# Split activations for TensorE: from high and low parts side by side to one block of low parts and one block of high parts

## The chip, the cores and the metric

The kernel runs on one core of a Trainium2 chip. The metric is the device time of one execution in microseconds. Before the change the median of three runs is 1348.29 us (1348.04 to 1348.34). A profiled execution took 1349.55 us, and the rows below are of that one.

## The reference

A sequence of 256 tokens with 1024 features goes through one layer of a first network and two layers of a second one, all in float32, batch 1. Cut to the parts that hold the large products:

```python
# first network, one layer
h = rmsnorm(x, g_mix);  z = h @ w_in            # 1024 -> 3232, split into latents, q, k, v, gates
ya, yb = two attentions over z ...              # projected by w_oa, w_ob
x = x + (sigmoid(gate_a) * ya + sigmoid(gate_b) * yb) @ w_o
u = relu(rmsnorm(x, g_mlp) @ w_up);  x = x + (u * u) @ w_down        # 1024 -> 4096 -> 1024
x = x + sigmoid(rmsnorm(x, g_ple) @ w_ple_gate) * (p @ w_ple)
x = rmsnorm(x, g_final)
# second network, two layers; the feed-forward runs before and after each mixer
def swiglu(h, w_in, w_out):
    a, b = split(h @ w_in, 2);  return (silu(a) * b) @ w_out         # 1024 -> 2 x 2816 -> 1024
for layer in range(2):
    x = x + 0.5 * swiglu(rmsnorm_2(x), ...)
    x = x + (even_mixer or odd_mixer)(rmsnorm_2(x), ...)
    x = x + 0.5 * swiglu(rmsnorm_2(x), ...)
out = rmsnorm_2(x, final_norm_g)
```

## The kernel before, in words

Products keep float32 accuracy with TensorE's fp32r type in three passes. Every weight block is loaded in float32 into `raw` by the SP queue, rounded by ScalarE into a high part `whi` (line 1278) and the rest is written by VectorE as a low part `wlo` (line 1734). Four slots of 2048 columns of each are held. Activations are split alike, into high parts (`hh`) and low parts (`hl`), and a product is the sum of high times high, high times low and low times high; low times low is left out.

The activations that enter the wide layers are held transposed, in the tile `hx`: eight blocks k of 128 features, 256 tokens each. Before the change the high part of block k is followed at once by its low part, so that both are one run of 512 columns: `hx` is `[128, 8, 2, 256]`. ScalarE writes the high parts (lines 1304, 1464 and 1540), VectorE the low ones (lines 1764, 1998 and 2126). The tiles are placed one after the other in each partition: `whi` and `wlo` begin at a multiple of 512 B, `hx` 64 B behind one (the tile `pad_hx` of 16 floats, line 204), and `ra`, which holds other activations, at a multiple of 512 B again (`pad_ra`).

TensorE's program is written out by hand, in one order, with waits on semaphores; each matmul is issued by `mm` (line 466), the transposes by `tp` (line 475). A matmul has a stationary operand (128 by 128, loaded by an LDWEIGHTS of its own) and a moving operand (128 rows by 128 to 512 columns). `hx` is read in three ways:

- `up_part` (lines 502 to 520), for the layers 1024 to 4096 and 1024 to 2 x 2816. For each of two groups f of 128 outputs and eight blocks k, a **wide pass** keeps a block of `whi` stationary and moves high and low parts of block k together, 512 columns, into the PSUM bank of f. Then, for the same f and k, a **correction pass** keeps the block of `wlo` stationary and moves the high part alone, 256 columns, onto the columns of the bank that hold the high products. VectorE adds the bank's two halves of 256 columns with a reduction (`hi_and_lo`, line 1834). A call of all eight blocks has 16 wide and 16 correction passes. With `behind=1` (the second of two calls in a feed-forward step) the last wide pass stands behind the correction passes.
- `gemm_b`, `b_part`, `by_steps` and two short loops: a **triple** of passes with weights stationary, moving 256 columns each: `whi` with `hh`, `whi` with `hl`, `wlo` with `hh`.
- `gemm_a` and its like: `hx` is stationary, in a triple `hh`, `hh`, `hl`, and weights move, mostly 512 columns.

A step of a feed-forward layer is one or two calls of `up_part`, then `down`: 24 passes with a piece of `ra` stationary and 512 columns of weights moving. In these layers wide passes, correction passes and `down` follow each other all the time. The split of later weights, the reductions and the activation functions run on the other engines beside them.

Of the kernel before, what the change touches and what calls it, by code (L numbers as in the profile page):

```python
# [7 lines left out]
R = mybir.dt.float32r  # L8
# [4 lines left out]
S = 256  # L13
# [150 lines left out]
def program(nc, W, XIN, XT, PT_IN, CST, GNS, GQK, GFIN, GFIN2, GLAG, FOXB, T5, OUT):  # L164
# [22 lines left out]
    with ExitStack() as ctx:  # L187
        def sb(name, shape, dt=F):
            return ctx.enter_context(nc.sbuf_tensor(name, shape, dt))
# [5 lines left out]
        ps = [pp[:, i, :] for i in range(8)]  # L195
# [5 lines left out]
        sb("pad", [128, 120])  # L201
        whi = sb("whi", [128, NHL, CW], R)
        wlo = sb("wlo", [128, NHL, CW], R)
        sb("pad_hx", [128, 16])
        hx = sb("hx", [128, 8, 2, S], R)
        sb("pad_ra", [128, 112])
        ra = sb("ra", [128, 4096], R)
        raw = sb("raw", [128, NRAW, HW])
        X = sb("X", [128, 2, D])
# [66 lines left out]
        def two(a):  # L276
            return a.rearrange("p (h c) -> p h c", h=2)

        def flat(a):
            return a.rearrange("p r c -> p (r c)")  # L280
# [20 lines left out]
            i, c, n = halves[j]  # L301
            return wlo[:, i % NHL, c:c + n]

        hh, hl = hx[:, :, 0, :], hx[:, :, 1, :]
        xT = fx[:, :].rearrange("p (k c) -> p k c", k=8)
        ACC = [[0, 1], [2, 3]]
        accs = [[ps[b][:, :] for b in r] for r in ACC]
# [156 lines left out]
        def tensor_program(pe):  # L464
            def mm(o, lhs, rhs, first, last):
                return pe.matmul(o, lhs, rhs, start=first, stop=last, skip_group_check=True)  # L466
# [35 lines left out]
            def up_part(tag, b, ks, norm=None, behind=0):  # L502
                i = IDX[tag]
                s = i % NHL
                wide = [(f, k) for f in range(2) for k in ks]

                def both(f, k, last):
                    c = k * 256 + f * 128
                    return mm(ps[b + f][:, :], whi[:, s, c:c + 128], flat(hx[:, k, :, :]), k == 0, last)

                for f, k in wide[:len(wide) - behind]:
                    if f == 0 and norm is not None:
                        pe.wait_ge(s_hl, 8 * norm + k + 1)
                    both(f, k, False)
                for f, k in wide:
                    c = k * 256 + f * 128
                    y = mm(ps[b + f][:, 0:256], wlo[:, s, c:c + 128], hh[:, k, :], False, k == 7 and not (behind and f))
                for f, k in wide[len(wide) - behind:]:
                    y = both(f, k, k == 7)
                return y  # L520
# [58 lines left out]
            def opening(k, tags):  # L579
                ta, tb = tags  # L580
                pe.wait_ge(s_hl, 8 * k + 4)
                weights_ready(IDX[ta])
                if k == 3:
                    pe.wait_ge(s_pgt, 2)
                up_part(ta, 4, range(4))
                if k == 3:
                    weights_ready(IDX[tb])
                    pe.wait_ge(s_pgt, 4)
                    up_part(tb, 6, range(2))
                    join_turn(k, 1)  # L590
                    up_part(tb, 6, range(2, 4))
                else:
                    weights_ready(IDX[tb])
                    up_part(tb, 6, range(1))
                    join_turn(k, 1)
                    up_part(tb, 6, range(1, 4))
                up_part(ta, 4, range(4, 8), k).then_inc(s_done)
                if k not in (1, 3):
                    spread(k, 0)
                up_part(tb, 6, range(4, 8)).then_inc(s_done)  # L600
                if k == 3:
                    spread(k, 0)
# [2015 lines left out]
```

## Time and profile before

| | before |
|---|---|
| median of 3 runs | 1348.29 us |
| the profiled execution, its own time | 1349.55 us |
| its span from first to last instruction | 1347.5 us |
| granted TensorE clock, mean over the span | 0.997 |
| TensorE (PE) busy | 1331.7 us, 99% |
| weight loads (PEld) busy | 1143.9 us, 85% |
| VectorE (DVE) busy | 968.7 us, 72% |
| ScalarE (ACT) busy | 678.6 us, 50% |
| GpSimd (POOL) busy | 68.6 us, 5% |
| mean DMA rate | 179 GB/s |

How to read it: a matmul's start is recorded and its end is modelled, and matmuls overlap, so the mean duration of one (some 390 ns for 512 columns) is not what a pass costs. What it costs is the distance from its start to the start of the next. The timeline gives that: it merges equal neighbours, so a row with `x16`, and the start of the row behind it, give the time of 16 passes.

### The profile page before, as it was taken

The page shows a single profiled execution, that of the slowest core. Times are in us where ns is not written, and L with a number is a line of the kernel's source. Part 1 is how long each engine was busy: PE and PEld are TensorE (multiplying, and loading weights), DVE is VectorE, ACT ScalarE, POOL GpSimd, SP SyncE. Part 2 cuts the span into 40 slices and gives each one's busy share as a digit, 9 for nine tenths or more (in the row PEclk, how much of TensorE's full clock was granted, in tenths as well). Part 3 has the DMA queues.
Part 4 walks back from the last instruction along what each step waited for, and adds up shares of the span by engine and source line. Part 5 has one row for each costly group of instructions (what it writes and reads, how often), then busy time and mean ns, then how long its engine had stood idle before and what let it go on. Part 6 is the DMA issues. An engine that isn't in the chain of part 4 may idle for free.

```text
span 1347.5 us, 19411 instructions
## 1 busy us (share of the span) xinstructions
PE 1331.7 (99%) x7680; PEld 1143.9 (85%) x7680; DVE 968.7 (72%) x1325; ACT 678.6 (50%) x1058; POOL 68.6 (5%) x108
## 2 busy tenths in 40 slices
PE   8999999999999999999999999999999999999998
PEld 6988888888888888898888888888888887888886
DVE  6786777666687776657767777777676798676775
ACT  6587354444564444556654444544443667544442
POOL 0300010000000000004000000000000043000000
PEclk9999999999999999999999999999999999999999
DMA  9353546555536656564346555556555555566551
GB/s 336 113 167 116 184 163 232 196 193 190 187 121 217 198 194 195 160 203 120 133 156 218 189 195 193 173 191 200 194 196 167 176 146 147 173 204 204 188 188 47
DMA packets 67562, 241.24 MB, mean 179 GB/s; under 512 B 7983, under 2 KB 8376, under 8 KB 67472
## 3 DMA queue, kind: packets, MB, share of 16 engines
q1 hardware_dynamic: 65200, 234.19, 52.8%
q0 software_dynamic: 1984, 5.70, 1.8%
q8 instruction: 61, 1.00, 0.3%
q14 instruction: 29, 0.24, 0.1%
q10 hardware_dynamic: 288, 0.11, 0.0%
HBM read 238.88 MB, written 1.09 MB: 178 GB/s over the span
## 4 chain that ended last, share of the span: by engine, by line
PE 90%; DVE 6%; issue 1%; ACT 1%; DMA 1%; POOL 0%; DVEq 0%; POOLq 0%; SPq 0%; ACTq 0%
PE pp L466 87%; DVE wlo L1734 2%; PE pp L475 2%; DVE fa L1734 1%; DVE hx L1742 0%; DMA raw<-w_chunks 0%; DVE pbuf L1738 0%; ACT whi L1278 0%; DVE fa L1834 0%; DVE xn L1734 0%; ACT hx L1279 0%; DVE xn L1943 0%; DMA fa<-f_rows 0%; DVE fa L1742 0%; DMA f_rows<-fa 0%
## 5 line engine op out<-in xcount | busy, mean ns | idle before, releaser
L1734 DVE TENSOR_TENSOR wlo<-raw,whi 128x1024 fp32r<-128x1024 f32 (+1 forms) x444 | 523.1, 1220 | 139.0 <-ACT whi L1278 138.7
L466 PE MATMUL pp<-hx,whi 128*128 128x512 f32 (+1 forms) x2400 | 546.8, 360 | 2.1 <-DVE fa L1834 1.1
L1278 ACT ACTIVATE whi<-raw 128x1024 fp32r<-128x1024 f32 (+1 forms) x444 | 442.0, 1043 | 80.3 <-PE pp L466 72.9
L466 PEld LDWEIGHTS pp<-hx,whi 128*128 128x128 f32 x2400 | 419.5, 188 | 72.2 <-issue 7.9
L466 PE MATMUL pp<-whi,ra 128*128 128x512 f32 x1144 | 365.9, 391 | 0.5 <-issue 0.5
L466 PE MATMUL pp<-hx,wlo 128*128 128x256 f32 x2032 | 311.8, 277 | 0.0
L466 PEld LDWEIGHTS pp<-hx,wlo 128*128 128x128 f32 x2032 | 276.3, 188 | 10.1
L466 PEld LDWEIGHTS pp<-whi,ra 128*128 128x128 f32 x1144 | 214.6, 188 | 44.1 <-issue 1.6
L466 PE MATMUL pp<-wlo,ra 128*128 128x512 f32 x572 | 222.6, 389 | 0.0
L1834 DVE TENSOR_REDUCE fa<-pp 128x512 f32<-128x1024 f32 x104 | 127.0, 1221 | 72.6 <-PE pp L466 72.4
L1278 ACT ACTIVATE ra<-fa 128x512 fp32r<-128x512 f32 x63 | 39.8, 632 | 227.6 <-DVE fa L1742 227.6
L1374 ACT ACTIVATE fa<-fa 128x512 f32<-128x512 f32 x44 | 27.8, 632 | 194.6 <-DVE fa L1734 194.6
L466 PEld LDWEIGHTS pp<-wlo,ra 128*128 128x128 f32 x572 | 107.5, 188 | 21.3 <-issue 0.2
L466 PE MATMUL pp<-whi,hx 128*128 128x512 f32 (+2 forms) x320 | 95.6, 378 | 2.0 <-DVE wlo L1734 2.0
L1734 DVE TENSOR_TENSOR ra<-fa,ra 128x512 fp32r<-128x512 f32 x63 | 43.6, 693 | 43.3 <-ACT ra L1278 43.3
L2405 POOL TENSOR_TENSOR st<-st,cst 128x2 f32<-128x2 f32 (+3 forms) x15 | 13.4, 894 | 1180.7 <-DVE st L1739 1159.4
L466 PEld LDWEIGHTS pp<-whi,hx 128*128 128x128 f32 x320 | 58.8, 190 | 15.8 <-issue 4.1
L466 PE MATMUL pp<-wlo,hx 128*128 128x512 f32 (+2 forms) x160 | 60.1, 375 | 0.0
L1742 DVE SCALAR_TENSOR_TENSOR fa<-fa 128x512 f32<-128x512 f32 x65 | 44.5, 684 | 2.8 <-ACT fa L1625 0.7
L1742 DVE SCALAR_TENSOR_TENSOR hx<-pp,gns,hx 128x256 fp32r<-128x256 f32 x64 | 26.5, 477 | 23.1 <-ACT hx L1279 23.1
L1317 ACT ACTIVATE xn<-X 128x512 f32<-128x512 f32 x36 | 22.4, 627 | 28.4 <-DVE X L1742 28.1
L466 PEld LDWEIGHTS pp<-wlo,hx 128*128 128x128 f32 x160 | 30.5, 191 | 5.6
(176 smaller groups left out, 767.3 us busy)
## 6 DMA issues: line engine op xcount, KB each, us to landing
raw<-w_chunks SPq DMA_DIRECT2D x438, 512.0 KB, 5.2
fa<-t_rows POOLq DMA_DIRECT2D x16, 128.0 KB, 3.5
fx<-x_t SPq DMA_DIRECT2D x2, 512.0 KB, 6.5
X<-x_in SPq DMA_DIRECT2D x2, 512.0 KB, 7.4
fa<-g_fin POOLq DMA_DIRECT2D x2, 512.0 KB, 4.3
fa<-f_rows POOLq DMA_DIRECT2D x8, 128.0 KB, 3.2
raw<-w_chunks SPq DMA_DIRECT2D x3, 256.0 KB, 5.8
cst<-consts POOLq DMA_DIRECT2D x1, 576.0 KB, 7.4
```

The costliest lines, as they stand in the source:

```text
L466: return pe.matmul(o, lhs, rhs, start=first, stop=last, skip_group_check=True)
L475: return pe.transpose(o, src, ident[0:n, 0:n])
L1278: return act.activation(o, i, ACT.Copy, scale=1.0)
L1317: act.activation(xn[:, t, sl], X[:, t, sl], ACT.Square, scale=1.0, accum_out=st[:, q + 2 * c + t:q + 2 * c + t + 1]).then_inc(s_sq)
L1374: act.activation(fr[:, g % 2, :], fr[:, g % 2, :], ACT.Silu, scale=1.0).then_inc(s_silu)
L1734: return dve.tensor_tensor(o, a, b, op)
L1742: return dve.scalar_tensor_tensor(out=o, in0=a, scalar=s, in1=b, op0=op0, op1=op1)
L1834: return dve.tensor_reduce(two(o), pp[:, b:b + 2, :].rearrange("p f (s c) -> p f c s", s=2), AX.X, ALU.add)
L2405: return pool.tensor_tensor(o, a, C("mhalf")[:, 0:1].to_broadcast([128, n]), ALU.pow)
```

## The change

`hx` becomes `[128, 2, 2064]`: a block of all eight low parts (2048 floats), 16 floats of padding, then a block of all eight high parts. `pad_hx` goes and `pad_ra` shrinks by 16 floats, so that the block of low parts begins at a multiple of 512 B, the block of high parts 64 B behind one, and `ra` and all tiles behind it stay where they were. `hl` and `hh` become views of the two blocks. A wide pass now moves two runs of 256 columns, low part first, 8256 B apart, where it moved one run of 512. So the high products land in columns 256 to 511 of a bank, and the correction passes add onto these; the reduction adds the halves as before. No instruction is added, removed or moved on any engine. Where ScalarE and VectorE write two neighbouring blocks in one instruction (lines 1540 and 2126), two runs of 256 become one of 512.

```diff
--- before.py
+++ after.py
@@ -201,9 +201,8 @@
         sb("pad", [128, 120])
         whi = sb("whi", [128, NHL, CW], R)
         wlo = sb("wlo", [128, NHL, CW], R)
-        sb("pad_hx", [128, 16])
-        hx = sb("hx", [128, 8, 2, S], R)
-        sb("pad_ra", [128, 112])
+        hx = sb("hx", [128, 2, 8 * S + 16], R)
+        sb("pad_ra", [128, 96])
         ra = sb("ra", [128, 4096], R)
@@ -301,7 +300,7 @@
-        hh, hl = hx[:, :, 0, :], hx[:, :, 1, :]
+        hl, hh = [hx[:, i, 0:8 * S].rearrange("p (k c) -> p k c", k=8) for i in range(2)]
@@ -506,7 +505,7 @@
                 def both(f, k, last):
                     c = k * 256 + f * 128
-                    return mm(ps[b + f][:, :], whi[:, s, c:c + 128], flat(hx[:, k, :, :]), k == 0, last)
+                    return mm(two(ps[b + f][:, :]), whi[:, s, c:c + 128], hx[:, :, S * k:S * k + S], k == 0, last)
@@ -514,7 +513,7 @@
                 for f, k in wide:
                     c = k * 256 + f * 128
-                    y = mm(ps[b + f][:, 0:256], wlo[:, s, c:c + 128], hh[:, k, :], False, k == 7 and not (behind and f))
+                    y = mm(ps[b + f][:, 256:512], wlo[:, s, c:c + 128], hh[:, k, :], False, k == 7 and not (behind and f))
```

## Rows read from the trace of the kernel before

**Rows 1.** The page: busy time by engine, and the chain that ended last.

```profile
PE 1331.7 (99%) x7680; PEld 1143.9 (85%) x7680; DVE 968.7 (72%) x1325; ACT 678.6 (50%) x1058; POOL 68.6 (5%) x108
...
PE 90%; DVE 6%; issue 1%; ACT 1%; DMA 1%; POOL 0%; DVEq 0%; POOLq 0%; SPq 0%; ACTq 0%
```

**Rows 2.** Groups by form on PE: passes with `hx` (count; mean, idle before).

```profile
L466 PE MATMUL pp<-hx,whi 128*128 128x512 f32 x1664 | 408.8, 393 | 1.4 <-DVE fa L1834 1.1
...
L466 PE MATMUL pp<-hx,wlo 128*128 128x256 f32 x2032 | 311.8, 277 | 0.0
L466 PE MATMUL pp<-hx,whi 128*128 128x256 f32 x736 | 138.0, 287 | 0.7 <-DVE fx L1734 0.7
L466 PE MATMUL pp<-whi,hx 128*128 128x512 f32 x256 | 83.6, 401 | 2.0 <-DVE wlo L1734 2.0
```

**Rows 3.** Timeline of PE, a feed-forward step (start us, modelled us, what).

```profile
399.21 3.60 PE L466 MATMUL pp<-hx,whi 128*128 128x512 f32 x15
402.65 1.98 PE L466 MATMUL pp<-hx,wlo 128*128 128x256 f32 x16
404.46 0.39 PE L466 MATMUL pp<-hx,whi 128*128 128x512 f32 x1
404.69 0.39 PE L466 MATMUL pp<-whi,ra 128*128 128x512 f32 x1
...
405.60 0.39 PE L466 MATMUL pp<-wlo,ra 128*128 128x512 f32 x1
...
409.68 0.39 PE L466 MATMUL pp<-wlo,ra 128*128 128x512 f32 x1
...
410.14 3.84 PE L466 MATMUL pp<-hx,whi 128*128 128x512 f32 x16
413.82 1.98 PE L466 MATMUL pp<-hx,wlo 128*128 128x256 f32 x16
```

**Rows 4.** Timeline of PE: 16 correction passes at another price, and the next 16.

```profile
539.71 2.05 PE L466 MATMUL pp<-hx,wlo 128*128 128x256 f32 x16
541.59 3.61 PE L466 MATMUL pp<-hx,whi 128*128 128x512 f32 x15
545.04 1.98 PE L466 MATMUL pp<-hx,wlo 128*128 128x256 f32 x16
546.85 0.39 PE L466 MATMUL pp<-hx,whi 128*128 128x512 f32 x1
```

**Rows 5.** Timeline of PE: the last full series of 16 correction passes in the program.

```profile
1322.53 1.98 PE L466 MATMUL pp<-hx,wlo 128*128 128x256 f32 x16
1324.34 0.39 PE L466 MATMUL pp<-hx,whi 128*128 128x512 f32 x1
```

**Rows 6.** Timeline of PE: `ra` stationary, then triples that move `hx`.

```profile
60.07 0.39 PE L466 MATMUL pp<-whi,ra 128*128 128x512 f32 x1
60.30 0.40 PE L466 MATMUL pp<-hx,whi 128*128 128x256 f32 x2
...
61.01 0.40 PE L466 MATMUL pp<-hx,whi 128*128 128x256 f32 x2
...
62.07 0.40 PE L466 MATMUL pp<-hx,whi 128*128 128x256 f32 x2
```

**Rows 7.** Timeline of PE: triples that move `hx`, another place.

```profile
75.61 0.39 PE L466 MATMUL pp<-hx,whi 128*128 128x256 f32 x2
...
77.99 0.39 PE L466 MATMUL pp<-hx,whi 128*128 128x256 f32 x2
```

**Rows 8.** Timeline of PE: triples that move `ra`, 256 columns.

```profile
131.16 0.40 PE L466 MATMUL pp<-ra,whi 128*128 128x256 f32 x2
...
133.68 0.40 PE L466 MATMUL pp<-ra,whi 128*128 128x256 f32 x2
```

**Rows 9.** Timeline of PE: triples with `hx` stationary, weights moving.

```profile
351.16 0.63 PE L466 MATMUL pp<-whi,hx 128*128 128x512 f32 x2
...
353.26 0.63 PE L466 MATMUL pp<-whi,hx 128*128 128x512 f32 x2
```

## The prediction

> **What bounds the kernel now.** I read the busy times first, then the chain of waits, and then, since only one engine was left, the timeline of that engine. TensorE is busy 99% of the span and 90% of the chain that ended last is TensorE [rows 1]; the groups that read `hx` wait for others 2.1 us in all when their moving operand is `hx`, and 2.0 us in the largest where it is stationary [rows 2]. So the time is close to the sum of the distances between matmul starts, and nothing on the other engines covers a change in them. The change touches no instruction's place; it can act only through what a pass costs. That is why the timeline is read by starts: the modelled means of 277 to 401 ns [rows 2] say nothing of it.
>
> What the reader is to see in the timeline is that passes of one size have several prices, and that the price goes with where in a 512 B stretch of a partition the two operands begin.
>
> - Wide passes, `hx` moving 64 B behind a boundary, weights at one: (402.65 - 399.21) / 15 = 229.3 ns, and (413.82 - 410.14) / 16 = 230.0 ns [rows 3].
> - 512 columns of weights moving, `ra` stationary, both at a boundary: eighteen passes from 405.60 to 409.68, 226.7 ns [rows 3].
> - 512 columns of weights moving, `hx` stationary 64 B behind: nine passes from 351.16 to 353.26, 233.3 ns [rows 9].
> - 256 columns of `ra` moving, both at a boundary: 21 passes from 131.16 to 133.68, 120.0 ns [rows 8].
> - 256 columns of `hx` moving, 64 B behind: 113.3 ns in one place (21 passes, 75.61 to 77.99) [rows 7] and 117.8 in another (nine passes, 61.01 to 62.07) [rows 6].
>
> The last line matters most. Places and sizes are the same there, and the price is not. Correction passes show the same two prices: 16 in 1.81 us, 113.1 ns each (402.65 to 404.46) [rows 3], but 16 in 1.88 us, 117.5 ns each, at 539.71 [rows 4]. I count 94 full series of 16, 87 of them at the short price, from the first layer to the last one at 1322.53 [rows 5]. Nothing waits in the dear series, and the next series is cheap again (545.04 to 546.85, 1.81 us) [rows 4]. So a series settles into a short or a long beat, and which one depends on the moment at which it is entered. Inference, not shown by a row: the prices 113.3, 117.8, 120.0, 226.7 and 233.3 are all multiples of a third of 6.67 ns, as if starts were held to a common beat. The triples that follow passes with both operands at a boundary show the long beat: from 60.30 on 256-column passes of `hx` follow such a stretch without a gap, and go at 117.8 [rows 6].
>
> **The change part by part.** The sum is made against the profiled execution, 1349.55 us; the median of the runs, 1348.29, lies 1.26 us lower, and the forecast is moved down by that.
>
> Wide passes, 1664 [rows 2]. The first run of a pass is now the low part, at a boundary, and the next weights, at a boundary too, are loaded while it moves. The nearest row is then 226.7, the case with both at a boundary [rows 3]; the second run of columns comes when I expect that load to be over. No pass in this kernel moves two runs, so the seam has no row. Bounds: 226.7 below (no stretch of 512-column passes is faster) and above it two 256-column passes one after the other, 120.0 + 113.3 = 233.3 [rows 7, 8], which is also the dearest 512-column price seen [rows 9]. I take 226.7, since a seam inside an instruction should cost less than a second instruction with its own weights. From the mean of 229.3 and 230.0 that is 3.0 ns less: 1664 x 3.0 = 5.0 us gained; at the upper bound 3.6 ns more, 6.0 us lost.
>
> Correction passes. Their own operands keep their places (`hh` still 64 B behind). What moves is how a series is entered: today from wide passes of 229 to 230 ns, after it from passes like those of `ra`. The one place that shows 256-column passes of `hx` behind a settled stretch of that kind shows the long beat [rows 6]. I take it for all 87 series: 87 x (1.88 - 1.81) = 6.1 us lost [rows 3, 4]. The other end is 0.
>
> Triples that move `hx`: 736 passes with `whi`, so 368 triples [rows 2], whose middle pass moves to a boundary. Today 353 ns [rows 6] or 340 [rows 7]; with all passes at a boundary 360 [rows 8]. Ends: 368 x 7 = 2.6 us lost, 368 x 13 = 4.8 gained. One pass in three moves towards the 360 case: 0.8 us lost.
>
> Triples with `hx` stationary: 256 passes with `whi`, 128 triples of 512 columns [rows 2], of which the third has its stationary operand moved to a boundary. 700 ns now [rows 9]; if all three were there, 680 [rows 3]. Ends 0 and 128 x 20 = 2.6 us gained; a third of it, 0.9.
>
> Changeovers. The 24 passes behind an `up_part` take 5.45 us (404.69 to 410.14), against 24 x 226.7 = 5.44 [rows 3]; the 15 wide passes behind the dear series take 3.45 us [rows 4] against 3.44 [rows 3]. So settling costs some 0.01 us per call more behind a dear series: with 104 calls (1664 / 16) 1.0 us lost, ends 0 and 2.
>
> The writers of `hx` cost nothing: same count, same elements, beside TensorE. If that cover went, the chain of waits would show them: VectorE has 6% of it now [rows 1].
>
> Sum: -5.0 + 6.1 + 0.8 - 0.9 + 1.0 = +2.0 us: 1351.55 in the profiled execution's terms, **1350.3** as a median, 0.15% above 1348.29.
>
> A rule speaks for a plainer result. The Trainium skill, TensorE: Matmul & The Clock Gate, in "Step-by-step: what each phase is for", says that the array has two independent read ports into the on-chip memory, so that loading the next weights takes no read bandwidth from the running matmul. By this rule neither place nor order of the blocks would count, and the sum would be 0. The rows disagree as far as they go: one shape at 113.3, 117.8 and 120.0 ns [rows 6 to 8].
>
> **The rivals.**
>
> - **Only the gain** (25%). The wide passes go to 226.7 and the correction passes keep the short beat. For it: 87 of 94 series have it now. Against it: [rows 6]. -5.0 + 0.8 - 0.9 = -5.1 us, 1343.2. Faster.
> - **Only the loss** (17%). The wide passes stay at 229 to 230, the second run of columns giving back what the first gained, but their beat is another, so the series turn to the long one. +6.1 + 0.8 - 0.9 + 1.0 = +7.0 us, 1355.3. Slower. It decides at the entry of the series: from about 70 of 87 turned on, with nothing gained in the wide passes, the kernel is slower by over 0.2% even without the smaller terms (70 x 0.07 = 4.9 us).
> - **The seam costs** (15%). A wide pass pays for the jump like a second pass: 233.3, +6.0 us, 1354.2 with the short beat behind it; with the long one about +13, 1361. For it: no row with two runs exists. Against it: it would have to cost 6.6 ns beyond the 226.7 case.
> - **Nothing moves** (10%). Prices belong to something other than place, the change does not do what it says, and the two prices of one place [rows 6, 7] are the only sign. 0 +- 1.5 us, 1348.3.
>
> **How the numbers follow.** The forecast, gain and loss together, gets 33%, with +-1.5 us around 1350.3. A measurement of this kernel can tell about 0.2%, 2.7 us, from no change. Faster: the first rival, 25%, and 2% from the edges of others, 27%. Slower: 17% + 15% + the upper third of the forecast, 12%, makes 44%. Within: 29%. The range is 1342.5 to 1356.5: it reaches from the first rival's 1343.2 to just beyond 1355.3, and leaves out the seam with the long beat and gains below the 226.7 bound, under 20%.
>
> **What would show it.** In the timeline of the changed kernel: 16 wide passes in 3.63 us (226.7 each) show the first term right; 3.73 us show the seam; 3.67 us show that nothing moved. 16 correction passes in 1.88 us show the second term, 1.81 refute it. Triples of `hx` between 353 and 360 ns, and triples with `hx` stationary near 693 ns, show the small ones. The prediction is wrong if wide passes go below 226.7, if correction passes take a price that has no row here, or if TensorE's idle time grows by more than a microsecond.

## The result, and the profile after

The changed kernel takes 1361.00 us (median of 4 runs, 1360.49 to 1363.52) where the kernel before takes 1348.23 us beside it: a ratio of 1.0091, 95% interval 1.0079 to 1.0102. It is slower, by 12.8 us. The forecast was 1350.3 us with a range up to 1356.5, so the outcome given the largest chance, slower, came true and the size lies outside the range. The profiled execution took 1360.49 us with a span of 1358.4 us, against 1349.55 and 1347.5 before: 10.9 us between the two, which is what the rows below have to explain, as the profiled execution before lies 1.3 us above its median and the one after 0.5 us below; the mean granted clock is 0.999 against 0.997, so the clock is not the cause.

Line numbers are one lower after the change. The page of the changed kernel, busy time by engine and the chain that ended last:

```profile
PE 1343.3 (99%) x7680; PEld 1150.2 (85%) x7680; DVE 968.4 (71%) x1325; ACT 679.2 (50%) x1058; POOL 68.6 (5%) x108
...
PE 88%; DVE 6%; DMA 2%; ACT 2%; issue 1%; POOL 0%; SPq 0%; DVEq 0%; POOLq 0%; ACTq 0%
```

As in [rows 1], TensorE fills the span, and the other engines do the same work in the same time. Its waits did not grow either. The groups by form on PE of the changed kernel (count | busy us, mean ns of one | idle before):

```profile
L465 PE MATMUL pp<-hx,whi 128*128 128x512 f32 x1664 | 413.2, 395 | 1.2 <-DVE fa L1833 0.9
...
L465 PE MATMUL pp<-hx,wlo 128*128 128x256 f32 x2032 | 318.1, 279 | 0.0
L465 PE MATMUL pp<-hx,whi 128*128 128x256 f32 x736 | 139.4, 289 | 0.6 <-DVE fx L1733 0.6
L465 PE MATMUL pp<-whi,hx 128*128 128x512 f32 x256 | 82.7, 397 | 2.0 <-DVE wlo L1733 2.0
```

The idle times are those of [rows 2] or less. So all of it is in the distance from one matmul start to the next. The same feed-forward step as in [rows 3], timeline of PE after the change (start us, modelled us, what):

```profile
400.01 3.66 PE L465 MATMUL pp<-hx,whi 128*128 128x512 f32 x15
403.51 2.05 PE L465 MATMUL pp<-hx,wlo 128*128 128x256 f32 x16
405.40 0.39 PE L465 MATMUL pp<-hx,whi 128*128 128x512 f32 x1
405.63 0.39 PE L465 MATMUL pp<-whi,ra 128*128 128x512 f32 x1
...
411.12 3.88 PE L465 MATMUL pp<-hx,whi 128*128 128x512 f32 x16
```

- 15 wide passes take 403.51 - 400.01 = 3.50 us, 233.3 ns each; before 3.44 us, 229.3.
- 16 correction passes take 405.40 - 403.51 = 1.89 us, the long beat; before 1.81.
- The 24 passes with `ra` stationary take 411.12 - 405.63 = 5.49 us; before 5.45.

The two small kinds, timeline of the changed kernel: triples that move `hx`, then triples with `hx` stationary:

```profile
60.07 0.41 PE L465 MATMUL pp<-hx,whi 128*128 128x256 f32 x2
...
62.21 0.41 PE L465 MATMUL pp<-hx,whi 128*128 128x256 f32 x2
...
351.78 0.63 PE L465 MATMUL pp<-whi,hx 128*128 128x512 f32 x2
...
353.18 0.63 PE L465 MATMUL pp<-whi,hx 128*128 128x512 f32 x2
```

18 passes in 2.14 us are 118.9 ns each (117.8 in [rows 6], 113.3 in [rows 7]); six passes in 1.40 us are 233.3 ns, as in [rows 9].

To get totals I added up the distances between successive starts over the whole trace, by kind, leaving out those that hold a wait (the row of the corrections is the sum of all 1664):

| kind | before | after | difference |
|---|---|---|---|
| wide passes, mean | 229.6 ns | 232.2 ns | +4.3 us |
| corrections of `up_part` (1664) | 191.8 us | 197.7 us | +5.9 us |
| `ra` stationary, mean of 1679 | 227.5 ns | 228.2 ns | +1.3 us |
| triples moving `hx`, mean of 1104 passes | 117.4 ns | 118.7 ns | +1.5 us |
| `hx` stationary, mean | 233.4 ns | 232.8 ns | -0.2 us |

That is +12.8 us; the long distances, which hold the waits, give back 1.7 us. The sum, 11.1 us, stands against 10.9 us of span. Of the 94 full series of 16 corrections, 87 had the short beat before; in the changed kernel none has.

### The profile page after: what moved, and what is told of

It is laid out like the page before. It is cut to its first block, busy times and chain, and to the rows that moved or that the text cites. A ratio compares the mean times of both kernels' runs of the same rounds, so it can differ in the third digit from the quotient of the medians.

```text
span 1358.4 us, 19411 instructions
## 1 busy us (share of the span) xinstructions
PE 1343.3 (99%) x7680; PEld 1150.2 (85%) x7680; DVE 968.4 (71%) x1325; ACT 679.2 (50%) x1058; POOL 68.6 (5%) x108
## 4 chain that ended last, share of the span: by engine, by line
PE 88%; DVE 6%; DMA 2%; ACT 2%; issue 1%; POOL 0%; SPq 0%; DVEq 0%; POOLq 0%; ACTq 0%
PE pp L465 86%; DVE wlo L1733 3%; PE pp L474 2%; DMA raw<-w_chunks 2%; DVE fa L1733 1%; DVE hx L1741 1%; ACT whi L1277 1%; DVE pbuf L1737 0%; DVE xn L1733 0%; DVE fa L1833 0%; ACT hx L1278 0%; DVE xn L1942 0%; DVE fa L1741 0%; DMA fa<-f_rows 0%; ACT fa L1278 0%
## 5 line engine op out<-in xcount | busy, mean ns | idle before, releaser
L465 PE MATMUL pp<-hx,whi 128*128 128x512 f32 (+1 forms) x2400 | 552.5, 363 | 1.8 <-DVE fa L1833 0.9
L465 PE MATMUL pp<-hx,wlo 128*128 128x256 f32 x2032 | 318.1, 279 | 0.0
L465 PEld LDWEIGHTS pp<-hx,wlo 128*128 128x128 f32 x2032 | 281.6, 188 | 10.6
L1733 DVE TENSOR_TENSOR fa<-fa,rbb 128x512 f32<-128x512 f32 x47 | 32.4, 692 | 3.5 <-ACT fa L1613 1.1
```

Source lines behind the costliest of these rows:

```text
L1733: return dve.tensor_tensor(o, a, b, op)
```

## The experiments

Two things had to be explained: why the wide passes became dearer, although the nearest row promised 226.7 ns, and why the corrections, whose operands did not move, turned to the long beat. Ratios are to the kernel before, run on the same chip. "Wide" and "correction" prices without another source are means over the whole trace, added up as above.

### Two runs, without a change of place

The changed kernel, with both blocks 64 B behind a boundary.

```diff
-        hx = sb("hx", [128, 2, 8 * S + 16], R)
-        sb("pad_ra", [128, 96])
+        sb("pad_hx", [128, 16])
+        hx = sb("hx", [128, 2, 8 * S], R)
+        sb("pad_ra", [128, 112])
```

> Two blocks, low parts first, but both 64 B behind a 512 B boundary: the wide pass still moves two runs, and within a 512 B stretch their places are those of the kernel before. Theory J (the jump of 64 B between the two runs costs the 2.6 ns a wide pass): wide passes as before, 229.7 ns, correction passes mostly 113.3, 1348.2 us +-1.5. Theory B (a first run at the boundary, beside the load of the next weights, costs it): the same, 1348.2. Theory F (moving two runs costs by itself, wherever they lie): wide passes 232.3 or more, correction passes 117.8, 1358 to 1361 us.

1350.14 us against 1349.74, ratio 1.0001 (0.9992 to 1.0010). Timeline of PE, start of a step:

```profile
306.10 3.84 PE L466 MATMUL pp<-hx,whi 128*128 128x512 f32 x16
309.79 1.98 PE L466 MATMUL pp<-hx,wlo 128*128 128x256 f32 x16
311.60 0.39 PE L466 MATMUL pp<-whi,ra 128*128 128x512 f32 x1
```

Wide passes 229.6 ns on average, as before; corrections 1.81 us for 16, and 192.1 us in all against 191.8. Theory F falls: moving two runs 8192 B apart in one instruction, low part first and with the other half of the bank for the high products, costs nothing by itself. With it the seam rival falls in the form in which it was told. What remains is where the runs start.

### Both blocks at the boundary, in two runs and in one

The same with no padding ahead of `hx`; and, as a second kernel, the layout before (one run of 512) with no padding.

```diff
-        hx = sb("hx", [128, 2, 8 * S + 16], R)
-        sb("pad_ra", [128, 96])
+        hx = sb("hx", [128, 2, 8 * S], R)
+        sb("pad_ra", [128, 128])
```

```diff
-        sb("pad_hx", [128, 16])
         hx = sb("hx", [128, 8, 2, S], R)
-        sb("pad_ra", [128, 112])
+        sb("pad_ra", [128, 128])
```

> Two blocks, low parts first, both at a 512 B boundary. Theory J: wide passes at 226.7 ns, as with ra stationary; correction passes and triples move the high parts from a boundary and take 120.0 ns: 1664 x -3.0 + 1664 x 4.7 + 368 x 7 ns = -5.0 + 7.8 + 2.6, so 1353.6 us. Theory B: wide passes stay at 232.3 ns: 1663 us is not meant, but 1348.2 + 4.3 + 7.8 + 2.6 = 1362.9 us. Theory F: wide passes at 232 or more, 1363 us or more.

> The kernel before with hx moved to the 512 B boundary: one run of 512 columns, high part first, stationary hx at the boundary too. Theories J and F: wide passes at 226.7 ns, correction passes and triples at 120.0, 1353.6 us (less up to 2.6 us for hx stationary at the boundary). Theory B: wide passes at 232.3, 1362.9 us.

1355.90 us, 1.0042 (1.0026 to 1.0059), and 1355.31 us, 1.0039 (1.0026 to 1.0052). The two-run kernel's timeline of PE, at the start of a step and at triples with `hx` stationary:

```profile
305.87 3.79 PE L465 MATMUL pp<-hx,whi 128*128 128x512 f32 x16
309.50 2.08 PE L465 MATMUL pp<-hx,wlo 128*128 128x256 f32 x16
311.41 0.40 PE L465 MATMUL pp<-whi,ra 128*128 128x512 f32 x1
...
351.12 0.62 PE L465 MATMUL pp<-whi,hx 128*128 128x512 f32 x2
...
353.16 0.62 PE L465 MATMUL pp<-whi,hx 128*128 128x512 f32 x2
```

The same step of the one-run kernel:

```profile
306.07 3.79 PE L465 MATMUL pp<-hx,whi 128*128 128x512 f32 x16
309.70 2.08 PE L465 MATMUL pp<-hx,wlo 128*128 128x256 f32 x16
311.61 0.40 PE L465 MATMUL pp<-whi,ra 128*128 128x512 f32 x1
```

In the two-run kernel the 16 wide passes take 3.63 us, 226.9 each; 16 corrections 1.91 us, 119.4; nine passes with `hx` stationary 2.04 us, 226.7. The one-run kernel has the same 3.63 and 1.91 us. Theories B and F fall. So the row read for the first term was a good guide to a place: with everything at the boundary wide passes do go at 226.7, in one run or two; the mean over the trace is 227.9, as the first five passes behind a series of corrections take 228 to 237 ns. Corrections then pay some 120 ns, as the `ra` triples of [rows 8] do, and they lose more than the wide passes win: -2.7 + 8.8 us in the two-run kernel, with +1.7 for triples and -2.2 for `hx` stationary (differences of all distances, waits included; the span is 5.4 us longer). Both places alone are cheaper for a wide pass (227.9 and 229.6 on average) than the changed kernel's mixture of the two (232.2).

### Both blocks moved on by 64 B

Low parts 64 B behind a boundary, high parts 128 B.

```diff
-        hx = sb("hx", [128, 2, 8 * S + 16], R)
-        sb("pad_ra", [128, 96])
+        sb("pad_hx", [128, 16])
+        hx = sb("hx", [128, 2, 8 * S + 16], R)
+        sb("pad_ra", [128, 80])
```

> The changed kernel with both blocks moved 64 B on: low parts 64 B behind a boundary, high parts 128 B. The jump of 64 B stays, the first run leaves the boundary. Theory J: wide passes stay near 232.3 ns. Theory B: back to 229.7 ns. Theory F: 232.3 or more. For the correction passes, which now move from 128 B, no row has a price: between 113.3 and 120.0 ns. Time 1348 to 1362 us.

1363.10 us, 1.0095 (1.0079 to 1.0112). Timeline of PE:

```profile
307.19 3.90 PE L466 MATMUL pp<-hx,whi 128*128 128x512 f32 x16
310.93 2.06 PE L466 MATMUL pp<-hx,wlo 128*128 128x256 f32 x16
312.82 0.40 PE L466 MATMUL pp<-whi,ra 128*128 128x512 f32 x1
```

Wide passes 3.74 us for 16, 232.9 ns on average: theory B falls once more, and the time lies just above the range expected. I read this at first as the price of the jump of 64 B between the runs, wherever they start. The last four runs, below, weaken that: 128 B is a dear place without any jump.

### Half of the changes of place taken out

In the changed kernel, odd blocks k move the high part first, so that a pass begins in the place where the one before it ended. For these k the products of high and low parts trade halves of the bank; the reduction adds both halves, so the sum is the same.

```diff
+                    w = hx[:, :, S * k:S * k + S]
+                    if k % 2:
+                        at0 = hx[:, 1, S * k:S * k + S]
+                        w = bass.AP(at0.tensor, at0.offset, [list(at0.ap[0]), [-(8 * S + 16), 2], [1, S]])
```

> The changed kernel, but for odd k a wide pass moves the high part first and then the low part (the sum over the two halves of a bank is the same). The places in a 512 B stretch then go 0, 64 | 64, 0 | 0, 64: the jump between the two runs of a pass stays, the jump back between two passes goes. Theory J-in (the jump inside a pass costs): wide passes near 232.3 ns as in the changed kernel. Theory J-border (the jump back at the border of two passes costs): 226.7 to 229.7 ns, 4 to 9 us less in the wide passes, so about 1352 to 1357 us.

1356.88 us, 1.0055 (1.0038 to 1.0072). Timeline of PE:

```profile
306.35 3.83 PE L465 MATMUL pp<-hx,whi 128*128 128x512 f32 x16
310.02 2.05 PE L465 MATMUL pp<-hx,wlo 128*128 128x256 f32 x16
311.90 0.40 PE L465 MATMUL pp<-whi,ra 128*128 128x512 f32 x1
```

The same step of the changed kernel:

```profile
306.31 3.88 PE L465 MATMUL pp<-hx,whi 128*128 128x512 f32 x16
310.03 2.05 PE L465 MATMUL pp<-hx,wlo 128*128 128x256 f32 x16
```

16 wide passes in 3.67 us, where the changed kernel has 3.72. Over the trace the average is 230.1 ns, between what the two theories of the jump expected, and half way from the changed kernel's 232.2 to the 227.9 of both blocks at the boundary. The same places in the same mixture, with fewer changes from one to the other, cost 2.1 ns less. It is not the direction of the jump inside a pass that decides: in the trace of this run, in full calls and without the first pass of each, the passes that move the low part first have a mean of 229.8 ns and those that move the high part first 229.5. So the run ties the extra price of this mixture to the number of changes between 0 and 64 B. That a change inside a pass costs as much as one between two passes is not shown.

### The high block 256 B behind

```diff
-        hx = sb("hx", [128, 2, 8 * S + 16], R)
-        sb("pad_ra", [128, 96])
+        hx = sb("hx", [128, 2, 8 * S + 64], R)
```

> The changed kernel with the block of high parts 256 B behind a boundary, not 64. Theory J (any jump inside the pass that is no multiple of 512 B costs): wide passes above 229.7 ns, 230 to 235. Theory J64 (only a start 64 B behind meets something): wide passes at 226.7. Correction passes and triples now move from 256 B, which has no row: 113.3 to 120.0 ns. Time 1348 to 1363 us.

1355.78 us, 1.0045 (1.0030 to 1.0060). Timeline of PE:

```profile
305.95 3.79 PE L464 MATMUL pp<-hx,whi 128*128 128x512 f32 x16
309.57 2.08 PE L464 MATMUL pp<-hx,wlo 128*128 128x256 f32 x16
311.49 0.40 PE L464 MATMUL pp<-whi,ra 128*128 128x512 f32 x1
```

3.62 and 1.92 us: the prices of both blocks at the boundary. A start at 256 B counts here as one at 0, and changing between those two costs nothing. So theory J in this form, that every jump off a multiple of 512 B costs, falls. Theory J64 told the price of this run, but the run with the high block at 128 B, below, takes it back: a start 64 B behind is not the only dear one.

### The entry of the corrections: the kernel before, with one pass moved

No tile is moved. The last wide pass of every full call stands behind the corrections, as it did in the second call of a feed-forward step already.

```diff
-                    up_part(f"up{g}", 4 + 2 * (g % 2), range(8)).then_inc(s_done)
+                    up_part(f"up{g}", 4 + 2 * (g % 2), range(8), behind=1).then_inc(s_done)
...
-                    up_part(f"{a}{g}", 4, range(8)).then_inc(s_done)
+                    up_part(f"{a}{g}", 4, range(8), behind=1).then_inc(s_done)
```

> The kernel before, with no tile moved; in every full call of up_part the last wide pass stands behind the correction passes (behind=1 also for the first layer's calls and the first call of a step). Only what runs ahead of a series of correction passes changes: 15 wide passes where it was 16. Theory N (a series takes its price, 113.3 or 117.8 ns, from how it is entered): most of the series that change turn to 117.8; with 54 to 94 series turned, 4 to 6.5 us more, 1352.2 to 1354.7 us, wide passes near 229.7. Theory P (the price belongs to the place of the operands): all series stay as they were, 1348.2 us +-1.

1355.46 us against 1349.24, 1.0043 (1.0028 to 1.0058). Timeline of PE:

```profile
305.23 3.61 PE L466 MATMUL pp<-hx,whi 128*128 128x512 f32 x15
308.68 2.05 PE L466 MATMUL pp<-hx,wlo 128*128 128x256 f32 x16
310.57 0.40 PE L466 MATMUL pp<-hx,whi 128*128 128x512 f32 x1
```

Wide passes stay near their price (229.9 ns on average, 229.6 before), but 16 corrections now take 1.89 us: over the trace 1554 of 1664 lie at 116 ns or above, where 259 did, and 6 of the 94 full series are short, where 87 were. That is +5.2 us in the corrections with every operand in its place: theory N holds, theory P falls, and the time lies just above the range expected. It is not the number of wide passes alone that decides: the series in [rows 3] at 402.65 is short behind 15 wide passes that follow other corrections, and here one behind 15 that follow passes with `ra` stationary is long.

### The entry varied in the changed kernel

Between 9 and 16 wide passes ahead of the corrections, the rest behind them.

```diff
-                    up_part(f"{a}{g}", 4, range(8)).then_inc(s_done)
+                    up_part(f"{a}{g}", 4, range(8), behind=g % 8).then_inc(s_done)
...
-                    up_part(f"{b}{g}", 6, range(8), behind=1).then_inc(s_done)
+                    up_part(f"{b}{g}", 6, range(8), behind=(g + 4) % 8).then_inc(s_done)
```

The calls tagged `up` got `behind=g % 8` as well.

> The changed kernel, no tile moved, with 0 to 7 of the 16 wide passes of a call behind its correction passes, by turns. Theory N (the price of a series is set by how it is entered): among eight kinds of entry some series take 113.3 ns a pass, where the changed kernel has nearly all at 117.8. Theory P (the price belongs to the place): all stay at 117.8. Wide passes near 232.3 ns in either; 1355 to 1362 us.

1359.48 us, 1.0075 (1.0060 to 1.0090). Timeline of PE, three calls of one layer:

```profile
305.89 2.72 PE L465 MATMUL pp<-hx,whi 128*128 128x512 f32 x11
308.45 1.98 PE L465 MATMUL pp<-hx,wlo 128*128 128x256 f32 x16
310.26 1.32 PE L465 MATMUL pp<-hx,whi 128*128 128x512 f32 x5
...
316.90 2.48 PE L465 MATMUL pp<-hx,whi 128*128 128x512 f32 x10
319.22 2.05 PE L465 MATMUL pp<-hx,wlo 128*128 128x256 f32 x16
321.11 1.56 PE L465 MATMUL pp<-hx,whi 128*128 128x512 f32 x6
...
327.99 2.25 PE L465 MATMUL pp<-hx,whi 128*128 128x512 f32 x9
330.08 1.98 PE L465 MATMUL pp<-hx,wlo 128*128 128x256 f32 x16
331.90 1.80 PE L465 MATMUL pp<-hx,whi 128*128 128x512 f32 x7
```

Behind 11 and 9 wide passes the 16 corrections take 1.81 and 1.82 us, behind 10 they take 1.89, in one kernel with one layout. This repeats: all six series behind 11 passes and all six behind 9 are short, all six behind 10 long. In all, 17 of 94 full series are short, where the changed kernel has none, and 318 of 1664 corrections lie below 116 ns, where it has 49. The entry picks the beat; a full remedy this was not, as 77 series stay long.

### Other places

Three times the layout before, one run of 512, at 32, 128 and 192 B behind a boundary (`pad_hx` of 8, 32 and 48 floats, `pad_ra` shrunk to match); and the changed kernel with the high block 128 B behind the boundary (rows of `8 * S + 32` floats).

> The kernel before with hx 32 B behind a 512 B boundary in place of 64 B (one run of 512 columns, nothing else moved). Theory G (the price follows where the start lies in a stretch of 128 B or more, in steps finer than 64 B): 32 B has a price of its own, wide passes between the 226.7 ns of 0 B and the 229.6 ns of 64 B, corrections between 120.0 and 113.3, time anywhere from 1349 to 1356 us. Theory H (two classes only, at a multiple of 256 B or not): as the kernel before, 1349 us, 229.6 and 113.3 ns. Theory M (only a start at a multiple of 64 B has the short beat of the corrections): corrections 117.8 or 120, 1355 us.

> The kernel before with hx 128 B behind a 512 B boundary. The run with the high block 256 B behind showed that 256 B acts as 0. If the pattern repeats every 128 B, this is the run with hx at the boundary once more: wide passes 226.7 ns, corrections 120.0, 1355.3 us. If it repeats only every 256 B, 128 B has its own price; theory H (boundary of 256 B or not) says as before, 1349 us, 229.6 and 113.3 ns.

> The kernel before with hx 192 B behind a 512 B boundary. If the pattern repeats every 128 B, 192 B is 64 B: 229.6 and 113.3 ns, 1349 us, no difference. If every 256 B, it may have a price of its own; theory H says as before as well, so this run speaks only where it differs from the kernel before.

> The changed kernel with the high block 128 B behind a boundary in place of 64 B. If the pattern repeats every 128 B, the jump in a wide pass costs nothing here, as the one of 256 B did: wide passes 226.7 ns, corrections 120.0, 1355.8 us. If it repeats every 256 B only, the jump costs as that of 64 B or otherwise: wide passes 232 to 233 ns, corrections at 117.8 or below, 1356 to 1363 us. Below 1348 us only if the wide passes take 226.7 and the corrections 113.3 at once, for which no run so far speaks.

In this order: 1359.65 us, 1.0071 (1.0056 to 1.0086); 1363.76 us, 1.0098 (1.0083 to 1.0113); 1356.21 us, 1.0040 (1.0026 to 1.0054); 1363.33 us, 1.0096 (1.0081 to 1.0111). Timeline of PE with `hx` at 192 B, the one with news in the corrections:

```profile
306.79 3.89 PE L466 MATMUL pp<-hx,whi 128*128 128x512 f32 x16
310.53 1.99 PE L466 MATMUL pp<-hx,wlo 128*128 128x256 f32 x16
312.35 0.39 PE L466 MATMUL pp<-whi,ra 128*128 128x512 f32 x1
```

The table has all layouts (starts of low and high part behind a boundary; the flat ones have both parts in one run, where the second starts 1024 B on); prices are means over the trace.

| layout | wide, ns | corrections, us in all | ratio |
|---|---|---|---|
| flat 64 (before) | 229.6 | 191.8 | 1 |
| two runs, 64 and 64 | 229.6 | 192.1 | 1.0001 |
| flat 0 | 227.9 | 200.6 | 1.0039 |
| two runs, 0 and 0 | 227.9 | 200.6 | 1.0042 |
| two runs, 0 and 256 | 228.0 | 200.6 | 1.0045 |
| two runs, 0 and 64 (the change) | 232.2 | 197.7 | 1.0091 |
| the same, alternating | 230.1 | 197.7 | 1.0055 |
| two runs, 64 and 128 | 232.9 | 198.8 | 1.0095 |
| two runs, 0 and 128 | 233.0 | 198.8 | 1.0096 |
| flat 32 | 233.2 | 197.1 | 1.0071 |
| flat 128 | 232.8 | 199.9 | 1.0098 |
| flat 192 | 233.2 | 194.6 | 1.0040 |

128 B is neither as 0 nor as 64 B, flat or behind a block at 0, and 192 B is not as 64 B, so a repeat every 128 B falls in three runs. A repeat every 256 B agrees with the run at 256 B, but no other pair of places 256 B apart was tried. 32, 128 and 192 B are not as 64 B, so "at a multiple of 256 B or not" falls as well. At 32 B the price of 233.2 ns lies outside the bracket that theory G gave, and the time above it; theory M comes near on the corrections there (series of 116.7 to 117.9 ns a pass) and has no word on the wide passes. No layout has wide passes at 226.7 and corrections at 113.3, and no version beats the kernel before.

## Why the prediction was wrong

- **What bounds the kernel**: right. Engines and instruction order are as before, waits no longer, and the difference is made of distances between starts.
- **Wide passes: the step that failed.** The prediction took "the nearest row", 226.7 ns, because the first run starts at a boundary, and held a seam to be cheaper than a pass of its own. Measured: 232.2 ns, +4.3 us where -5.0 was put down, so this term missed by 9.3 us. Between profiled executions, in which the sum was made, the forecast missed by 8.9 us (1360.49 against 1351.55); the small terms and the shorter waits all but cancel. Between medians it missed by 10.7. The upper bound, 233.3, was sound and holds the value. The row was right for passes with both runs at the boundary, shown by two kernels; the error was to give a pass the price of its first run. This mixture of two places was dearer than either.
- **Corrections: right in size, and in that the entry decides; not for the reason given.** +6.1 us forecast, +5.9 measured, and all 87 series turned, to 1.88 or 1.89 us. That another entry turns them with their own operands in place is shown from both sides: series turned long with no operand moved, and some turned short again in the changed layout. But the forecast expected the long beat behind wide passes at 226.7 ns, "passes like those of `ra`". Such passes never came; those ahead took 232.2 ns. [rows 6] was thus not the case that was met, and that all the series turned even so was in part luck. So was the sign of the whole: one of the two large terms had the wrong one.
- **Small terms.** Triples that move `hx`: +0.8 forecast, +1.5 measured. `hx` stationary: -0.9 forecast, -0.2 measured. Changeovers: +1.0 forecast; the passes with `ra` stationary behind them cost 1.3 us more. All lie within their ends.
- **The range: a second failure, in "How the numbers follow".** The outcome was written down, "with the long one about +13, 1361", and then left out. The seam rival was priced with the short beat behind it, although the argument for the long one, another entry, held for it as much as for the forecast. With that counted, the range should have reached at least 1361.
- **Rule and trace.** Wide passes at 227.9 to 233.2 ns on average, with one run of 512 columns and nothing changed but where `hx` starts, speak against the conclusion that the prediction drew from the Trainium skill, TensorE: Matmul & The Clock Gate, "Step-by-step: what each phase is for": that with two independent read ports no place has a price. The measurement decides against this conclusion; that section of the Trainium skill says nothing of places. Whether the ports meet, or something else holds the starts to a beat, no run here shows.

Still open is a rule that gives the price of a place, and so why a mixture of 0 and 64 B is dearer than both. The alternating run ties it to the number of changes of place; the run at 64 and 128 B cannot, since 128 B is dear without a change. Open too is what in an entry picks the beat: the runs show that it changes, not by which rule.

## What to carry to other kernels

Where one engine runs back to back, the start of an operand can be worth a few ns a pass, here 0.4 to 1% of the time, and it has to be measured as a whole layout: the price of 0 and 64 B mixed was not found between the prices of the two. Ask of any such change what follows the altered passes, too, since the next series may fall into another beat with nothing of its own changed. And when two rivals share a cause, price them together before leaving their sum out of a range.

## What the runs showed of the hardware that was not expected

- Two runs 8192 B apart, both 64 B behind a boundary, cost a matmul's moving operand nothing (229.6 ns either way, ratio 1.0001).
- With one layout of the weights, the mean of a 512-column pass went from 227.9 to 233.2 ns by the start of `hx` alone, without order: 0, 64, then 128, 32 and 192 B. With 192 B, half of the corrections (786 of 1664) were below 116 ns and the triples that move `hx` at 115.2 ns, the cheapest of all layouts, beside one of the dearest wide passes.
- `hx` as the stationary operand was cheaper at a boundary too: 226.7 ns against 233.3.
- One pass more or fewer ahead of a series set the price of the 16 behind it: 1.81 us behind 11, 1.89 behind 10, 1.82 behind 9, the same in all six series of each kind.
